# Two 64-row block sums of an fp32 decoder layer: one full fp32 product or two fp32r passes

## The chip, the cores and the metric

The kernel runs on one core of one Trainium2 chip. The metric is the device time of one execution in microseconds (us); lower is better.

## What is computed

One decoder layer for a sequence of 256 tokens with 2048 channels, all in float32: an input projection, sixteen RWKV-7 heads of width 64 beside eight differential attention heads, an output projection, a layer norm, an MLP of width 8192 with squared ReLU, and a second layer norm. Two lines of the RWKV part matter here, both of them sums over the 64 channels of a head:

```
kk    = heads(k * k_k)
kk    = kk / jnp.maximum(jnp.sqrt(jnp.sum(jnp.square(kk), -1, keepdims=True)), 1e-12)
bonus = (jnp.sum(r_h * k_h * r_k, -1, keepdims=True) * v_h).reshape(B, S, RWKV_WIDTH)
```

## The kernel before

Channels lie on the 128 partitions and tokens along the free axis. So one block of 128 channels holds two heads, and a sum over a head's channels is a TensorE product with a 128x128 matrix `BD` of ones in its two diagonal 64x64 blocks. `BD` is a part of the float32 constants `cst`.

The big products are done as fp32r products of parts. Each slab of weights (1 MB, 128x2048 float32) is loaded by SP's queue into one of four `stage` buffers. ScalarE copies it rounded to fp32r into `whi` (function `hi`), and VectorE writes the remainder `stage - whi` into `wlo` (function `lo`). TensorE then multiplies the activations' rounded part and remainder (`acts`) by `whi` in a product of 512 columns, and the rounded activations by `wlo` in one of 256 columns (function `both`). There are two `whi` and two `wlo` buffers, so `hi` of slab g waits until TensorE has used slab g-2 (`s_used`).

The change lies in the stage that projects k, r and v. It is a loop of NB // 2 = 4 turns `j`, each with three groups `c`: c = 0 projects 256 channels of k, c = 1 of r, c = 2 of v. A group is `pairs(...)`: two slabs of 16 pairs of products each, some 11.5 us of TensorE. Its sums go to two PSUM banks, and groups take turns between two sets of banks. After the pairs of c = 1 TensorE makes the block sum of the kk squares (`sqt`), and after the pairs of c = 2 that of the bonus terms (`rkt_`). Every engine works through its own list in program order:

- ScalarE, per group m: `hi(g + 2)`; for c = 1 the two squares into `sqt`; for c = 2 the square root of the kk sums into `inv`; then `low_copied(m)`, which waits for the end of the group's pairs and copies half of the sums into `hs`; `hi(g + 3)`; two scaled copies of `hs` into `krv`.
- VectorE, per group: for c = 0 (from j = 1) `bonus_and_kk(j - 1)`; for c = 1 the factors `ki` and `bt`; for c = 2 the products `rkt_`; then `lo(g + 2)`; for c = 2 the maximum with 1e-12 (L1619) and a reciprocal of half of `inv` (L1621); `halves_added(m)` (L1587), `lo(g + 3)` and the token shift into `krv` (L1628), which gives `s_free`.
- GpSimd, once per turn: four products (L2053 to L2057) as soon as kk is ready.

The order of these steps is written out by hand, with semaphores. TensorE's matmuls are nearly all recorded at L475, ScalarE's instructions at L1148, and `lo` at L1502, so rows are told apart by their tiles. A full float32 matmul appears as two records (x2).

Of the kernel before, what the change touches and what calls it, by code (L numbers as in the profile page):

```python
# [8 lines left out]
ALU = mybir.AluOpType  # L9
ACT = mybir.ActivationFunctionType  # L10
F32 = mybir.dt.float32
F32R = mybir.dt.float32r
# [4 lines left out]
P = 128  # L17
D = 2048
S = 256
# [86 lines left out]
def build(nc, t):  # L106

    ctx = ExitStack()
    with ctx:
# [3 lines left out]
        def at(name, slot, shape, dtype=F32, byte=0):  # L113
            return nc.alloc_sbuf_tensor_at(name, shape, dtype, offset=BASE + slot * SL_BYTES + byte)
# [4 lines left out]
        def sem(name):  # L119
            return ctx.enter_context(nc.semaphore(name))  # L120
# [26 lines left out]
        sqt = at("sqt", 13, [P, 2, S])  # L147
        inv = at("inv", 13, [P, 2, S], byte=2048)
        rkt_ = at("rkt_", 13, [P, 2, S], byte=4096)
        yt = at("yt", 13, [P, NB, S])  # L150
        oshi = [at("oshi0", 16, [P, NB, S], F32R), at("oshi1", 14, [P, NB, S], F32R)]
        oslo = [at("oslo0", 17, [P, NB, S], F32R), at("oslo1", 15, [P, NB, S], F32R)]
# [74 lines left out]
        ps = ctx.enter_context(nc.psum_tensor("ps", [P, 8, 512], F32))  # L227
# [18 lines left out]
        s_sq, s_ss, s_nrm = sem("kk_squares"), sem("kk_sums"), sem("kk_norms")  # L246
        s_ew = sem("elementwise_step")
        s_rk, s_bon, s_kk, s_pl = sem("bonus_terms"), sem("bonus_sums"), sem("kk_ready"), sem("pool_step")
        s_bonv = sem("bonus_ready")
        s_vdc = sem("v_copied")  # L250
        s_lamd = sem("lambda_step")
        s_lame = sem("lambda_exps")
# [40 lines left out]
        def col(v, n=0):  # L293
            return vec[:, v + n:v + n + 1]
# [9 lines left out]
        def f(ap):  # L304
            return ap.bitcast(F32)

        SU, IU, ID = cst[:, C_SU:C_SU + P], cst[:, C_IU:C_IU + P], cst[:, C_ID:C_ID + P]
        BD = cst[:, C_BD:C_BD + P]
# [6 lines left out]
        def banks(a, n=2, lo=0, hi=512):  # L315
            return ps[:, a:a + n, lo:hi]
# [156 lines left out]
        def _(pe):  # L473
            def mm(out, lhsT, rhs, start=True, stop=True):
                return pe.matmul(out, lhsT, rhs, start=start, stop=stop, skip_group_check=True)  # L475
# [11 lines left out]
            def pairs(b0, g, k0):  # L487
                for s in range(2):
                    halves_ready(g + s)
                    for j in range(8):  # L490
                        for fb in range(2):
                            last = both(b0 + fb, (k0 + s) % NHL, slice(256 * j + fb * P, 256 * j + fb * P + P), 8 * s + j)
                    last.then_inc(s_used, 1)
# [55 lines left out]
            for p in range(NB // 2):  # L549
# [4 lines left out]
                        last = mm(ps[:, 4 + p, o:o + P], sig[:, a, P * b:P * b + P], IU)  # L554
                last.then_inc(s_item, 1)

            for j in range(NB // 2):
                for c in range(3):
                    m = 3 * j + c
                    pe.wait_ge(s_free, m + 1)  # L560
                    pairs(2 * (m % 2), G_MIX + 2 * m, G_MIX + 2 * m)
                    if c == 1:
                        pe.wait_ge(s_sq, j + 1)
                        mm(ps[:, 4 + j % 2, :], BD, sqt[:, :, :]).then_inc(s_ss, 1)
                    if c == 2:
                        pe.wait_ge(s_rk, j + 1)
                        mm(ps[:, 6 + j % 2, :], BD, rkt_[:, :, :]).then_inc(s_bon, 1)

            def pairs_by_head(s, bk, left, right):

# [575 lines left out]
        def _(act):  # L1146
            def A(out, in_, func, **kw):
                return act.activation(out, in_, func, **kw)  # L1148
# [49 lines left out]
            for p in range(NB // 2):  # L1198
# [6 lines left out]
                  ACT.Exp, scale=-DECAY)  # L1205
                A(e2[:, two, :].rearrange("p b q -> p (b q)"), ps[:, 4 + p, :], ACT.Exp, scale=DECAY).then_inc(s_itemd, 1)

            def sines():
                act.wait_ge(s_ang, 9)
                A(sinb[:, :], angt[0][:, :], ACT.Sin).then_inc(s_sin, 1)  # L1210
                A(cosb[:, :], angt[2][:, :], ACT.Sin).then_inc(s_sin, 1)

            def low_copied(m):
                act.wait_ge(s_used, G_MIX + 2 * m + 2)
                act.wait_ge(s_free, m + 2)
                A(hs[:, :, :], banks(2 * (m % 2), 2, S, 2 * S), ACT.Copy).then_inc(s_plow, 1)

            for j in range(NB // 2):
                for c in range(3):
                    m = 3 * j + c  # L1220
                    g = G_MIX + 2 * m
                    if m == 0:
                        act.wait_ge(s_hi, g + 2)
                    hi(g + 2, g + 2)
                    if m == 0:
                        sines()
                    if c == 1:
                        act.wait_ge(s_free, m + 2)
                        for b in (2 * j, 2 * j + 1):
                            last = A(sqt[:, b % 2, :], krv[:, b, :], ACT.Square, scale=col(V_KK, b))  # L1230
                        last.then_inc(s_sq, 1)
                    if c == 2:
                        act.wait_ge(s_ss, j + 1)
                        A(inv[:, :, :].rearrange("p b q -> p (b q)"), ps[:, 4 + j % 2, :], ACT.Sqrt).then_inc(s_nrm, 1)
                    low_copied(m)
                    hi(g + 3, g + 3)
                    act.wait_ge(s_psum, m + 1)
                    for fb in range(2):
                        blk = NB * c + 2 * j + fb
                        last = A(krv[:, blk, :], hs[:, fb, :], ACT.Copy, scale=col(V_OMMU, blk))  # L1240
                    last.then_inc(s_mix, 1)
# [252 lines left out]
        def _(dve):  # L1494
            TTn, TS, STT = dve.tensor_tensor, dve.tensor_scalar, dve.scalar_tensor_tensor
# [45 lines left out]
            n = 0  # L1541
# [31 lines left out]
            def bonus_and_kk(j):  # L1573
# [3 lines left out]
                for b in (2 * j, 2 * j + 1):  # L1577
# [4 lines left out]
                TTn(krv[:, NB + 2 * j:NB + 2 * j + 2, :], krv[:, 2 * NB + 2 * j:2 * NB + 2 * j + 2, :],  # L1582
                    ps[:, 6 + j % 2, :].rearrange("p (b q) -> p b q", b=2), ALU.mult).then_inc(s_bonv, 1)

            def halves_added(m):
                dve.wait_ge(s_plow, m + 1)
                TTn(hs[:, :, :], banks(2 * (m % 2), 2, 0, S), hs[:, :, :], ALU.add).then_inc(s_psum, 1)  # L1587

            for j in range(NB // 2):
                two = slice(2 * j, 2 * j + 2)  # L1590
                K, R, E = krv[:, two, :], krv[:, NB + 2 * j:NB + 2 * j + 2, :], 5 * j
                for c in range(3):
                    m = 3 * j + c
                    g = G_MIX + 2 * m
                    if c == 0 and j:
                        bonus_and_kk(j - 1)
                    if c == 1:
                        for b in (2 * j, 2 * j + 1):
                            last = TS(ki[:, b, :], bt[:, b, :], col(V_KA, b), col(V_OMKA, b), ALU.mult, ALU.add)
                        last.then_inc(s_ew, 1)  # L1600
                        dve.wait_ge(s_ew, E + 1)
                        TS(bt[:, two, :], bt[:, two, :], -1.0, None, ALU.mult)
                        dve.wait_ge(s_free, m + 2)
                        TTn(ki[:, two, :], K, ki[:, two, :], ALU.mult).then_inc(s_ew, 1)
                    if c == 2:
                        dve.wait_ge(s_ew, E + 2)
                        dve.wait_ge(s_free, m + 2)
                        for b in (2 * j, 2 * j + 1):
                            last = STT(rkt_[:, b % 2, :], krv[:, NB + b, :], col(V_RK, b), ki[:, b, :], ALU.mult, ALU.mult)
                        last.then_inc(s_rk, 1)  # L1610
                        rt = kr[:, two, :, 1, :]
                        TTn(rt, rt, R.rearrange("p b (a q) -> p b a q", a=TT_), ALU.mult)
                    lo(g + 2, g + 2)
                    if m == 0:
                        dve.wait_ge(s_sin, 2)
                        TS(sinb[:, :], sinb[:, :], col(V_SIGN), None, ALU.mult).then_inc(s_tab, 1)
                    if c == 2:
                        dve.wait_ge(s_nrm, j + 1)
                        TS(inv[:, :, :], inv[:, :, :], 1e-12, None, ALU.max).then_inc(s_ew, 1)  # L1619
                        dve.wait_ge(s_ew, E + 3)  # L1620
                        dve.reciprocal(inv[:, 0, :], inv[:, 0, :]).then_inc(s_ew, 1)  # L1621
                    halves_added(m)
                    lo(g + 3, g + 3)
                    dve.wait_ge(s_mix, m + 3)
                    for fb in range(2):
                        blk = NB * c + 2 * j + fb
                        out = krv[:, blk, 1:S]
                        last = STT(out, hs[:, fb, 0:S - 1], col(V_MU, blk), out, ALU.mult, ALU.add)  # L1628
                    last.then_inc(s_free, 1)
# [43 lines left out]
            for q in range(1, 2 * N_QK):  # L1673
# [12 lines left out]
                if q % 2 == 0:  # L1686
                    rotary(q // 2 - 1)
            halves_added(N_MIX - 1)
            lo(G_VD + 1, G_VD + 1)
            rotary(N_QK - 1)  # L1690
# [466 lines left out]
```

## Time and profile before

| what | value |
|---|---|
| device time, median of 3 runs | 1275.46 us |
| lowest and highest run | 1270.92 and 1276.71 us |
| profiled execution, span from first to last instruction | 1273.7 us |
| profiled execution, device time beside its span | not listed apart from the three runs |
| share of the span busy: TensorE, VectorE, ScalarE, GpSimd | 98%, 59%, 45%, 6% |
| granted TensorE clock, mean | 0.997 |

The profiled execution's span lies 1.8 us below the median of the three runs and between the lowest and the highest, so a sum made against its rows can be carried to the median as it is. "PE" is TensorE's matmuls, "PEld" its weight loads, DVE is VectorE, ACT is ScalarE, POOL is GpSimd. A busy time of PE counts modelled ends of matmuls that overlap, so the time that a matmul takes from the array is read from start to start, not from its duration.

### The profile page before, as it was taken

How to read it: one execution, taken by the hardware profiler on the slowest of the kernel's cores; microseconds unless marked ns; L12 is line 12 of the kernel's file. 1: busy time of each engine (PE TensorE's matmuls, PEld its weight loads, DVE VectorE, ACT ScalarE, POOL GpSimd, SP SyncE). 2: the span in 40 equal slices, each digit the busy share in tenths (PEclk: the TensorE clock that was granted, in tenths of full speed). 3: DMA queues.
4: the chain of work that ended last, by engine and by line, in shares of the span. 5: the costliest groups of instructions: out<-in, count | busy, mean ns of one | idle time of the engine just before them, and what ended most of it. 6: DMA issues, size and time to landing. Idle time of an engine off the chain costs nothing.

```text
span 1273.7 us, 23270 instructions
## 1 busy us (share of the span) xinstructions
PE 1248.1 (98%) x9644; PEld 1043.1 (82%) x9644; DVE 755.2 (59%) x806; ACT 570.2 (45%) x605; POOL 74.6 (6%) x44
## 2 busy tenths in 40 slices
PE   6999999999999899999999999999999999999997
PEld 6888888888789778888888888888888888888885
DVE  4577878465766265765554545555555555655557
ACT  4754445555656134434334343343444444444442
POOL 0022112000000000056000000000000000000000
PEclk9999999999999999999999999999999999999999
DMA  8355565333421426635555555555575555555541
GB/s 334 129 190 181 176 227 201 106 134 101 166 100 39 152 93 222 262 100 193 174 193 186 179 196 179 183 196 173 191 264 188 181 191 198 198 190 182 190 163 66
DMA packets 33506, 221.88 MB, mean 174 GB/s; under 512 B 4621, under 2 KB 5005, under 8 KB 7582
## 3 DMA queue, kind: packets, MB, share of 16 engines
q1 hardware_dynamic: 33438, 220.88, 50.0%
q8 instruction: 54, 0.88, 0.3%
q14 instruction: 14, 0.11, 0.0%
HBM read 218.77 MB, written 2.10 MB: 173 GB/s over the span
## 4 chain that ended last, share of the span: by engine, by line
PE 55%; DVE 1%; ACT 0%; issue 0%; DVEq 0%
PE ps L475 55%; DVE stats L1894 0%; DVE xres L1893 0%; DVE xres L2015 0%; DVE xres L2013 0%; DVE xres L2003 0%; ACT xres L1148 0%; DVE xres L2007 0%; DVE moments L1897 0%; DVE moments L1904 0%; ACT moments L1148 0%; DVE shift_diag L2029 0%; DVE moments L1903 0%; DVEq L1887 0%
## 5 line engine op out<-in xcount | busy, mean ns | idle before, releaser
L1502 DVE TENSOR_TENSOR wlo<-stage,whi 128x2048 fp32r<-128x2048 f32 x186 | 435.4, 2341 | 397.4 <-ACT whi L1148 396.9
L475 PE MATMUL ps<-acts,whi 128*128 128x512 f32 (+1 forms) x1792 | 620.1, 395 | 13.7 <-DVE wlo L1502 11.4
L1148 ACT ACTIVATE whi<-stage 128x2048 fp32r<-128x2048 f32 x193 | 369.7, 1917 | 505.4 <-PE ps L475 502.4
L475 PE MATMUL ps<-acts,wlo 128*128 128x256 f32 (+1 forms) x1744 | 486.3, 279 | 0.0
L475 PEld LDWEIGHTS ps<-acts,whi 128*128 128x128 f32 x1792 | 335.2, 189 | 93.1 <-issue 17.9
L475 PEld LDWEIGHTS ps<-acts,wlo 128*128 128x128 f32 x1744 | 330.6, 190 | 1.9 <-issue 1.9
L475 PE MATMUL ps<-whi,shi 128*128 128x512 f32 x504 | 198.0, 393 | 0.0
L475 PE MATMUL ps<-wlo,shi 128*128 128x512 f32 x504 | 196.5, 390 | 0.0
L475 PE MATMUL ps<-whi,slo 128*128 128x512 f32 x504 | 196.3, 389 | 0.0
L475 PEld LDWEIGHTS ps<-whi,shi 128*128 128x128 f32 x504 | 94.6, 188 | 26.5 <-issue 5.9
L475 PEld LDWEIGHTS ps<-wlo,shi 128*128 128x128 f32 x504 | 94.6, 188 | 20.3
L475 PEld LDWEIGHTS ps<-whi,slo 128*128 128x128 f32 x504 | 94.7, 188 | 18.1
L475 PE MATMUL ps<-whi,oshi 128*128 128x512 f32 x128 | 51.8, 405 | 0.0
L475 PE MATMUL ps<-whi,oslo 128*128 128x512 f32 x128 | 50.4, 394 | 0.0
L475 PE MATMUL ps<-wlo,oshi 128*128 128x512 f32 x128 | 50.4, 393 | 0.0
L1859 DVE TENSOR_TENSOR slo<-hid,shi 128x512 fp32r<-128x512 f32 x64 | 43.9, 685 | 0.0
L475 PE MATMUL ps<-whi,acts 128*128 128x512 f32 x128 | 41.1, 402 | 0.0
L1148 ACT ACTIVATE shi<-hid 128x512 fp32r (+1 forms) x64 | 39.2, 613 | 1.1 <-PE ps L475 1.1
L1148 ACT ACTIVATE TM_TT<-ps 128x512 f32<-128x512 f32 x36 | 19.8, 596 | 41.7 <-PE ps L475 41.7
L1587 DVE TENSOR_TENSOR hs<-ps,hs 128x512 f32<-128x512 f32 x20 | 13.6, 679 | 37.5 <-ACT hs L1148 37.4
L1148 ACT ACTIVATE hs<-ps 128x512 f32<-128x512 f32 x20 | 12.0, 599 | 49.1 <-PE ps L475 49.1
L2082 POOL TENSOR_TENSOR xres<-xres,gain 128x512 f32<-128x512 f32 x2 | 2.5, 1288 | 517.0 <-DVE slo L1859 517.0
(227 smaller groups left out, 986.0 us busy)
## 6 DMA issues: line engine op xcount, KB each, us to landing
stage<-w_ff SPq DMA_DIRECT2D x128, 1024.0 KB, 4.9
stage<-w_in SPq DMA_DIRECT2D x51, 1024.0 KB, 5.0
stage<-w_out SPq DMA_DIRECT2D x16, 1024.0 KB, 5.0
xstage<-xT SPq DMA_DIRECT2D x4, 512.0 KB, 7.1
TM_TT<-eyes SPq DMA_DIRECT2D x4, 512.0 KB, 7.6
xres<-x SPq DMA_DIRECT2D x1, 2048.0 KB, 9.7
gain<-ln_gain SPq DMA_DIRECT2D x2, 1024.0 KB, 6.9
bias<-ln_bias SPq DMA_DIRECT2D x2, 1024.0 KB, 9.6
```

Of the source, the lines that this page charges most:

```text
L475: return pe.matmul(out, lhsT, rhs, start=start, stop=stop, skip_group_check=True)
L1148: return act.activation(out, in_, func, **kw)
L1502: TTn(wlo[k0 % NHL][:, :], stage[k0 % NST][:, :], f(whi[k0 % NHL][:, :]), ALU.subtract).then_inc(s_lo, 1)
L1587: TTn(hs[:, :, :], banks(2 * (m % 2), 2, 0, S), hs[:, :, :], ALU.add).then_inc(s_psum, 1)
L1859: TTn(slo[h][:, :, :], src, f(shi[h][:, :, :]), ALU.subtract).then_inc(s_alo, 1)
L2082: PT(x, x, gain2[:, quarter(q)], ALU.mult).then_inc(s_pg, 1)
```

## The change

Each of the eight block sums becomes two fp32r passes that add up in PSUM: `bdr` x rounded summands, then `bdr` x remainders. `bdr` is an fp32r copy of `BD`, made once by ScalarE before the loop. For each sum ScalarE makes the rounded summands `sumh` (128x512) and VectorE the remainders `suml` (128x512); both buffers are used by all eight sums in turn. TensorE waits for both parts ahead of each sum.

```diff
+        sumh = at("sumh", 12, [P, 2, S], F32R)
+        suml = at("suml", 12, [P, 2, S], F32R, byte=5120)
+        bdr = at("bdr", 12, [P, P], F32R, byte=7168)
@@ TensorE
+            def block_sums(bank, n):
+
+                pe.wait_ge(s_smh, n)
+                pe.wait_ge(s_sml, n)
+                mm(ps[:, bank, :], bdr[:, :], sumh[:, :, :], stop=False)
+                return mm(ps[:, bank, :], bdr[:, :], suml[:, :, :], start=False)
+
                     if c == 1:
-                        pe.wait_ge(s_sq, j + 1)
-                        mm(ps[:, 4 + j % 2, :], BD, sqt[:, :, :]).then_inc(s_ss, 1)
+                        pe.wait_ge(s_bdr, 1)
+                        block_sums(4 + j % 2, 2 * j + 1).then_inc(s_ss, 1)
                     if c == 2:
-                        pe.wait_ge(s_rk, j + 1)
-                        mm(ps[:, 6 + j % 2, :], BD, rkt_[:, :, :]).then_inc(s_bon, 1)
+                        block_sums(6 + j % 2, 2 * j + 2).then_inc(s_bon, 1)
@@ ScalarE
+            A(bdr[:, :], BD, ACT.Copy).then_inc(s_bdr, 1)
...
                         last.then_inc(s_sq, 1)
+                        act.wait_ge(s_sq, j + 1)
+                        if j:
+                            act.wait_ge(s_bon, j)
+                        A(sumh[:, :, :], sqt[:, :, :], ACT.Copy).then_inc(s_smh, 1)
                     if c == 2:
                         act.wait_ge(s_ss, j + 1)
                         A(inv[:, :, :].rearrange("p b q -> p (b q)"), ps[:, 4 + j % 2, :], ACT.Sqrt).then_inc(s_nrm, 1)
+                        act.wait_ge(s_rk, j + 1)
+                        A(sumh[:, :, :], rkt_[:, :, :], ACT.Copy).then_inc(s_smh, 1)
@@ VectorE
+            def summands_lo(src, n, spent):
+                dve.wait_ge(s_smh, n)
+                if spent is not None:
+                    dve.wait_ge(*spent)
+                TTn(suml[:, :, :], src[:, :, :], f(sumh[:, :, :]), ALU.subtract).then_inc(s_sml, 1)
+
                         dve.reciprocal(inv[:, 0, :], inv[:, 0, :]).then_inc(s_ew, 1)
+                        summands_lo(rkt_, 2 * j + 2, (s_ss, j + 1))
+                    if c == 1:
+                        summands_lo(sqt, 2 * j + 1, (s_bon, j) if j else None)
                     halves_added(m)
```

## Rows read from the trace of the kernel before

**Rows 1.** The page: busy time by engine, and the chain that ended last.

```profile
PE 1248.1 (98%) x9644; PEld 1043.1 (82%) x9644; DVE 755.2 (59%) x806; ACT 570.2 (45%) x605; POOL 74.6 (6%) x44
...
PE 55%; DVE 1%; ACT 0%; issue 0%; DVEq 0%
```

**Rows 2.** Busy time of each engine in the stage of the k, r and v projections.

```profile
core 0: us, PE busy (x) PEld busy (x) DVE busy (x) ACT busy (x) POOL busy (x), PEclk, DMA share, GB/s
45.00:195.00 150.00, 149.62 (x942) 126.55 (x941) 114.45 (x115) 72.73 (x79) 26.55 (x14) 1.00 0.54 183
```

**Rows 3.** Timeline of PE (start, length) around the first kk sum.

```profile
64.36 1.02 PE L475 MATMUL ps<-sqt,cst 128*128 128x512 f32 x2
64.82 0.79 PE L475 MATMUL ps<-acts,whi 128*128 128x512 f32 x1
65.45 0.28 PE L475 MATMUL ps<-acts,wlo 128*128 128x256 f32 x1
```

**Rows 4.** Timeline of PE in the MLP's second product: 15 matmuls of 512 columns.

```profile
1133.63 0.39 PE L475 MATMUL ps<-whi,slo 128*128 128x512 f32 x1
...
1136.80 0.39 PE L475 MATMUL ps<-whi,shi 128*128 128x512 f32 x1
```

**Rows 5.** Timeline of PE: the first and the last of the four bonus sums.

```profile
76.32 1.02 PE L475 MATMUL ps<-rkt__82,cst 128*128 128x512 f32 x2
...
183.43 1.02 PE L475 MATMUL ps<-rkt__82,cst 128*128 128x512 f32 x2
```

**Rows 6.** Timeline of DVE around the same two bonus sums; in brackets idle time before.

```profile
75.64 1.75 DVE L1621 RECIPROCAL inv<-inv 128x256 f32<-128x256 f32 x1
77.31 0.63 DVE L1587 TENSOR_TENSOR hs<-ps,hs 128x512 f32<-128x512 f32 x1
78.95 2.29 DVE L1502 TENSOR_TENSOR wlo<-stage,whi 128x2048 fp32r<-128x2048 f32 x1 [1.01 <-ACT whi L1148]
...
182.76 1.75 DVE L1621 RECIPROCAL inv<-inv 128x256 f32<-128x256 f32 x1
184.43 0.63 DVE L1587 TENSOR_TENSOR hs<-ps,hs 128x512 f32<-128x512 f32 x1
```

**Rows 7.** Timeline of ACT ahead of the first bonus sum's end.

```profile
74.26 0.60 ACT L1148 ACTIVATE inv<-ps 128x512 f32<-128x512 f32 x1
76.52 0.60 ACT L1148 ACTIVATE hs<-ps 128x512 f32<-128x512 f32 x1 [1.66 <-PE ps L475]
```

**Rows 8.** Line L1859: a remainder of 128x512, min/median/max in ns.

```profile
L1859 DVE TENSOR_TENSOR slo<-hid,shi x64: 683/685/687, 901.9 to 1249.8; 128x512 fp32r<-128x512 f32 x64
```

**Rows 9.** Timelines of ACT, DVE and PE around the second kk sum.

```profile
96.30 0.89 ACT L1148 ACTIVATE sqt<-krv,vec 128x256 f32<-128x256 f32 x2
...
96.66 2.28 DVE L1502 TENSOR_TENSOR wlo<-stage,whi 128x2048 fp32r<-128x2048 f32 x1
...
99.87 1.02 PE L475 MATMUL ps<-sqt,cst 128*128 128x512 f32 x2
```

**Rows 10.** Timelines of POOL, DVE and PE in the second turn's group c = 0.

```profile
84.91 1.30 POOL L2053 TENSOR_TENSOR bt<-bt,krv  x1 [84.46 <-DVE krv L1578]
86.16 3.34 POOL L2054 TENSOR_TENSOR kr<-kr,krv  x1
...
85.13 3.22 DVE L1502 TENSOR_TENSOR wlo<-stage,whi 128x2048 fp32r<-128x2048 f32 x1
...
88.16 0.28 PE L475 MATMUL ps<-acts,wlo 128*128 128x256 f32 x1
88.50 0.47 PE L475 MATMUL ps<-acts,whi 128*128 128x512 f32 x1
88.81 0.28 PE L475 MATMUL ps<-acts,wlo 128*128 128x256 f32 x1
```

**Rows 11.** A gap of PE in the recurrence, and the clock granted after it.

```profile
420.85 0.27 PE L475 MATMUL ps<-um,btm 64*64 64x64 f32 x2 [2.02 <-issue]
...
426.00:429.40 3.40, 3.40 (x22) 2.24 (x18) 1.29 (x2) 0.00 (x0) 0.00 (x0) 0.51 0.82 282
```

More of the change, by code:

```diff
@@ L249, in build @@
         s_bonv = sem("bonus_ready")
+        s_bdr, s_smh, s_sml = sem("block_sums_rounded"), sem("summands_rounded"), sem("summands_remainders")
         s_vdc = sem("v_copied")
```

## The prediction

> **What bounds the kernel.** I read the page first. TensorE is busy 98% of the span, no other engine above 59%, and the chain that ended last runs through PE for 55% of the span, with nothing else above 1% [rows 1]. What the change touches is a stage of 150 us; its busy times by window show PE at 149.62 us of 150.00 while DVE has 35 us free, ACT 77 us and POOL more, at a granted clock of 1.00, the 2.4 GHz level [rows 2]. So here a microsecond counts when it is TensorE's. Extra work on ACT or DVE costs nothing until TensorE has to wait for its result. Then I read the timelines around the sums, engine by engine: the question is not how busy DVE is on average but whether it has the remainders ready when TensorE comes to the sum.
>
> **What a full fp32 sum costs now.** The first kk sum starts at 64.36. The matmul of 512 columns behind it is followed by the one of 256 columns at 65.45 [rows 3]. A plain matmul of 512 columns takes (1136.80 - 1133.63) / 14 = 0.226 us from start to start [rows 4], so without the sum the 256-column matmul would have come at 64.59. The sum takes 65.45 - 64.59 = 0.86 us from the array: four times 0.215, nearly four plain passes, though the trace shows two records.
>
> **What two passes cost.** 2 x 0.226 = 0.45 us. I find no fp32r block sum in this trace, but the passes have the shape of [rows 4]. Saving: 0.86 - 0.45 = 0.41 us a sum, 8 x 0.41 = 3.3 us if nothing waits. Bounds: no saving (an fp32r pass here as long as half of the old product), or 0.43 (exactly half). I take 0.41, by the nearest row. The Trainium skill (FP8 and Floating Point Precision, TensorE Precision Notes) says that a true FP32 product takes four passes through the array. By that rule two passes save half of 0.86, 0.43 us a sum and 3.4 us in all; the trace agrees to 0.02 us. On passes alone the change is a gain of 0.26%; the rule tells nothing of the two waits.
>
> **The copy of BD.** One ACT copy of 128x128 ahead of the loop, in a stretch in which ACT waits for PE before its next `hi`. Bound above by the copy of 128x512, 0.60 us [rows 7]; on the path: nothing. Uncovered it would delay the first `hi` by that much, once.
>
> **The kk sums (c = 1).** ACT adds a copy of 128x512 behind the squares, DVE a subtraction behind `lo(g + 2)`. Queued behind DVE's new wait are `halves_added` and `lo(g + 3)`. The tightest of the four turns is the second: the squares end at 96.30 + 0.89 = 97.19, and the copy (0.60) at 97.8. DVE's `lo` ends at 96.66 + 2.28 = 98.94, and the subtraction takes 0.685 [rows 8], to 99.62. TensorE comes to the sum at 99.87 [rows 9]. It is ready 0.25 us early, so these four sums bring their saving: 4 x 0.41 = 1.6 us. DVE stood idle there anyway until ACT's copy of the low halves, so `halves_added` isn't later.
>
> **The bonus sums (c = 2).** Here the order matters. The remainders are written behind `lo(g + 2)`, the maximum and a reciprocal of 1.75 us. TensorE is done with the pairs and comes to the sum at 76.32, but the reciprocal runs from 75.64 to 77.39, and the next DVE instruction starts at 77.31 [rows 5, 6]. The last turn has the same distances: sum at 183.43, next DVE instruction at 184.43; all four turns show 1.0 us. So the subtraction starts 1.0 us after TensorE wants its result, and takes 0.685: it ends at T + 1.68, with T the old start of the sum. Before, `rkt_` had been ready since long ahead, and the reciprocal hid behind the next group. Now four times TensorE stands still.
>
> The rounded part is not what is late: ACT ends the square root at 74.86, and its copy would end by 75.5, ahead of the copy of the low halves at 76.52 [rows 7].
>
> From the subtraction to TensorE's restart I look at the one place in the stage where PE waits for DVE: `lo` ends at 85.13 + 3.22 = 88.35, the matmul starts at 88.50 and the next one 0.31 later, not 0.226 [rows 10]. That is 0.15 + 0.08 us for a restart. The bounds are nothing and 0.23; I take 0.2. New cost of a bonus sum from T: 1.68 + 0.2 + 0.45 = 2.33 us, in place of 0.86. Loss: 1.47 us each, 5.9 us for four.
>
> What is late next: `halves_added(m)` moves from 77.31 to 78.0 and ends at 78.6. `lo(g + 3)` behind it started at 78.95 after an idle 1.01 us in wait for ACT's `hi` [rows 6], so it starts as before, and with it the token shift and kk. Nothing else moves, and TensorE has `lo(g + 2)` of its next group since 75.2. Without that idle time the 0.69 us would go to the next `lo`, not yet to TensorE, which wants that slab half a group later.
>
> **The group after it (c = 0).** `lo(g + 2)` took 3.22 us here, not 2.29, beside two POOL products (POOL's second took 3.34 where the first took 1.30), and TensorE waited: the step from 88.16 to 88.50 is 0.34, against 0.11 for a matmul of half 0.226 [rows 10]. That is 0.23 us in each of three turns. With TensorE 1.47 us later while kk and POOL keep their time, `hi` is released 1.47 us later and ends at about 86.35 (84.9 + 1.47), after POOL's second product has begun at 86.16. If `lo` then lasts 3.2 to 3.4 again it ends at 89.55 to 89.75, and TensorE wants it at 88.27 + 1.47 = 89.74. So most of the old wait is given back: between 0 and 3 x 0.23 = 0.7 us, I take 0.5. The Trainium skill (SBUF — State Buffer, SBUF: two separate sides) has VectorE and GpSimd take turns at a shared pair of ports, each for a whole instruction. By it `lo` would wait for POOL's second product, 1.3 us from 86.16 if undisturbed, and end at 87.46 + 2.29 = 89.75: the same answer.
>
> **Sum.** -1.6 (kk sums) + 5.9 (bonus sums) - 0.5 (the old waits) = +3.8 us. The ends of the unknowns: -1.6 + 4 x 1.27 - 0.7 = +2.8 with no cost of restart, and -1.6 + 4 x 1.5 = +4.4. The other 1079 us are not touched: they follow TensorE. Against the profiled execution: 1273.7 + 3.8 = 1277.5. It lies 1.8 us below the median, so the forecast is 1275.46 + 3.8 = 1279.3 us, +0.3%. No change that a measurement of this kernel tells from none: the three runs lie 0.45% apart, and I take 0.5% (6.4 us) as the limit.
>
> **Rivals.**
>
> 1. The saving comes whole: all eight sums are ready in time. Then 8 x -0.41 = -3.3 us: 1272.2 us, the other side. The place is the bonus sum. What decides is the time from TensorE's arrival to the end of the subtraction; the change as a whole gains if the standstill is under about 0.4 + (1.6 + 0.5) / 4 = 0.9 us, and it comes to 1.9. For it speaks that ACT and DVE are idle half of the time. Against it, the reciprocal ends 1.07 us after T in both of the turns shown, before any subtraction.
>
> 2. The clock falls in the standstills. Behind a stretch of the recurrence with a gap of 2.02 us the trace shows 3.4 us at a granted clock of 0.51, the 1.2 GHz level [rows 11], which costs 1.7 us. Four times that: +6.8, in all +10.6, 1286.1 us. For it: the gap has nearly the length of the new ones. Against it: there TensorE had small 64x64 products and a second gap before the clock fell; here it runs dense up to the wait and after it.
>
> 3. The kk sums wait too, if the two new instructions or their semaphores take over 0.25 us more than the rows say. At 0.5 us each: 4 x 0.5 = +2, 1281.3 us. Only the second turn is that tight.
>
> 4. An fp32r pass of the block sum costs as much as half of the old product in the array's time (no saving). Then the eight savings are lost, 3.3 us: +7.1, 1282.6 us. Against it, [rows 4].
>
> **Chances.** The forecast 0.76, rival 1 0.06, rival 2 0.07, rival 3 0.07, rival 4 0.04. The range: the runs of before lie 4.5 us below and 1.3 above their median, so a median of three can be off by some 3; around 1279.3 with ends at +2.8 and +4.4 that gives 1274 to 1283. I take 1273.5 to 1284.5, which takes in rivals 3 and 4. Faster by over 0.5% needs rival 1 and a low run: 0.03. Slower by over 0.5% (above 1281.8) comes from rivals 2 and 4, half of rival 3, and a high draw of the forecast: 0.07 + 0.04 + 0.03 + 0.06 = 0.20. Within: 0.77.
>
> **What would show it.** In the trace after: eight pairs of 512-column matmuls on `bdr`, 0.45 us of array time each; PE idle before the four on bonus terms for 1.7 to 1.9 us, released by DVE `suml`; none before the four on squares; DVE's `halves_added` of c = 2 0.69 us later but `lo(g + 3)` still waiting for ACT; the step of 0.34 before c = 1's first pair nearer to 0.11; clock 1.00 throughout the stage; the stage 3.8 us longer and all behind it merely moved. I am wrong if the subtraction runs ahead of the reciprocal's end, if the clock row of the stage falls under 1.00, or if a wait appears behind the stage.

## The result, and the profile after

The changed kernel takes 1280.04 us (median of 13 runs, 1278.57 to 1281.8); the kernel before, timed beside it, 1275.14 us (13 runs, 1267.47 to 1276.94). The ratio is 1.0043, with a 95% interval of 1.0032 to 1.0055: slower by 0.4%, less than the 0.5% set as the limit. The forecast was 1279.3 us.

The page of the changed kernel, busy time by engine:

```profile
span 1277.9 us, 23305 instructions
PE 1245.5 (97%) x9644; PEld 1042.8 (82%) x9644; DVE 755.7 (59%) x814; ACT 575.0 (45%) x614; POOL 71.6 (6%) x44
```

TensorE is busy 2.6 us less than in [rows 1] and the span is 4.2 us longer: it had less to do and stood still for longer. The waits of PE name a line that isn't there before (waiter, what it waited for, us in total, times, longest):

```profile
PE ps L479 <- DVE suml L1607: 6.4, 4, 1.6
```

Four waits of 1.6 us on the remainders. The timeline of PE at the first bonus sum, against [rows 5]:

```profile
75.42 0.28 PE L479 MATMUL ps<-acts,wlo 128*128 128x256 f32 x1
77.32 0.47 PE L479 MATMUL ps<-sumh,bdr 128*128 128x512 f32 x1 [1.61 <-DVE suml L1607]
77.62 0.40 PE L479 MATMUL ps<-suml,bdr 128*128 128x512 f32 x1
77.86 0.40 PE L479 MATMUL ps<-acts,whi 128*128 128x512 f32 x1
```

The last pair's 256 columns go in at 75.42, so TensorE comes to the sum at 75.54, 0.12 later, and starts it at 77.32: 1.78 us lost, of which the view calls 1.61 idle because it counts the modelled end of the matmul before. Then two passes, and the next group at 77.86: 2.32 us from arrival, where the full product took 0.86. DVE in the same stretch, against [rows 6]:

```profile
74.88 1.75 DVE L1645 RECIPROCAL inv<-inv 128x256 f32<-128x256 f32 x1
76.54 0.63 DVE L1607 TENSOR_TENSOR suml<-rkt__82,sumh 128x512 fp32r<-128x512 f32 x1
77.09 0.68 DVE L1611 TENSOR_TENSOR hs<-ps,hs 128x512 f32<-128x512 f32 x1
78.17 2.29 DVE L1520 TENSOR_TENSOR wlo<-stage,whi 128x2048 fp32r<-128x2048 f32 x1 [0.41 <-ACT whi L1158]
```

TensorE's wait lies under the second half of the reciprocal and the subtraction. The last line is the one to check for a knock-on: `lo` waits for ACT as before, only 0.41 us in place of 1.01. The rounded part was long there (timeline of ACT):

```profile
73.98 0.62 ACT L1158 ACTIVATE sumh<-rkt__82 128x512 fp32r<-128x512 f32 x1
75.74 0.60 ACT L1158 ACTIVATE hs<-ps 128x512 f32<-128x512 f32 x1 [1.13 <-PE ps L479]
```

And the first kk sum, on PE's timeline against [rows 3], with no wait:

```profile
63.86 0.28 PE L479 MATMUL ps<-acts,wlo 128*128 128x256 f32 x1
63.98 0.40 PE L479 MATMUL ps<-sumh,bdr 128*128 128x512 f32 x1
64.21 0.40 PE L479 MATMUL ps<-suml,bdr 128*128 128x512 f32 x1
64.44 0.39 PE L479 MATMUL ps<-acts,whi 128*128 128x512 f32 x1
```

**A ruler for the stage.** Single executions of one and the same kernel lie up to 12 us apart here (below), so a profile's span says little about a gain of 2 us. The stretch that the change touches can be measured by itself: from the start of the first kk sum to the first `bt,kr` product behind the last bonus sum. Before it goes from 64.36 [rows 3] to 190.62, after from 63.98 to 193.40 (PE's timelines; first line before, second after):

```profile
190.62 0.69 PE L475 MATMUL ps<-bt,kr 64*64 64x64 f32 x32
```

```profile
193.40 0.69 PE L479 MATMUL ps<-bt,kr 64*64 64x64 f32 x32
```

That is 126.26 us before and 129.42 after: +3.16 us. Below, "the stage" is this stretch.

### The profile page after: what moved, and what is told of

It is laid out like the page before. It is cut to its first block, busy times and chain, and to the rows that moved or that the text cites. A ratio compares the mean times of both kernels' runs of the same rounds, so it can differ in the third digit from the quotient of the medians.

```text
span 1277.9 us, 23305 instructions
## 1 busy us (share of the span) xinstructions
PE 1245.5 (97%) x9644; PEld 1042.8 (82%) x9644; DVE 755.7 (59%) x814; ACT 575.0 (45%) x614; POOL 71.6 (6%) x44
## 4 chain that ended last, share of the span: by engine, by line
PE 55%; DVE 1%; ACT 0%; issue 0%; DVEq 0%
PE ps L479 55%; DVE stats L1921 0%; DVE xres L1920 0%; DVE xres L2042 0%; DVE xres L2040 0%; DVE xres L2030 0%; ACT xres L1158 0%; DVE xres L2034 0%; DVE moments L1924 0%; DVE moments L1931 0%; ACT moments L1158 0%; DVE shift_diag L2056 0%; DVE moments L1930 0%; DVEq L1914 0%
```

## The experiments

### Where the loss is: one kind of sum at a time

`kk_sums_only`: the bonus sums stay full products.

```diff
-                        block_sums(6 + j % 2, 2 * j + 2).then_inc(s_bon, 1)
+                        pe.wait_ge(s_rk, j + 1)
+                        mm(ps[:, 6 + j % 2, :], BD, rkt_[:, :, :]).then_inc(s_bon, 1)
```

(and neither copy nor remainders for them; the semaphore counts follow)

> Only the four kk sums are two passes; the bonus sums stay full fp32 products, with no copy and no remainders for them. Theory: no wait on suml, 4 x -0.41 = -1.6 us against before, about 1273.5, the short waits beside GpSimd unchanged. Rival (the two-pass form costs something of its own): no gain or a loss.

`bonus_sums_only`: the kk sums stay full products.

```diff
-                        pe.wait_ge(s_bdr, 1)
-                        block_sums(4 + j % 2, 2 * j + 1).then_inc(s_ss, 1)
+                        pe.wait_ge(s_sq, j + 1)
+                        mm(ps[:, 4 + j % 2, :], BD, sqt[:, :, :]).then_inc(s_ss, 1)
```

(and neither copy nor remainders for the kk sums; the semaphore counts follow)

> Only the four bonus sums are two passes, with the remainders behind the reciprocal as in the changed kernel; the kk sums stay full fp32 products. Theory: the four waits of 1.8 us with the cheaper passes, 4 x 1.46 = +5.8, less 1.4 us of old waits beside GpSimd that go: +4.4 us by the trace's sum against before, or 1.6 us more than the changed kernel. Rival (half of the loss comes from the kk sums): about half of the changed kernel's +4.9, +2.5 us.

Measured: with the kk sums alone the ratio to before is 0.9975 (0.9956 to 0.9994), and the stage takes 188.12 - 63.52 = 124.60 us, 1.66 less than before, as 4 x 0.41 says. With the bonus sums alone the ratio is 1.0042 (1.0020 to 1.0064) and the stage 195.66 - 64.47 = 131.19 us, 4.93 more; the loss by ratio is 5.4 us, against 4.4 expected. Of the 0.5 us between 4.4 and 4.93 the expectation knew nothing; the last section finds it in matmuls that ran at a slower pace. The two parts add up to +3.27, and both together gave +3.16. So the whole loss is in the bonus sums, and the kk sums are a gain. The tile view of `suml` in the second run has no kk sums, and the same wait:

```profile
L1606 DVE TENSOR_TENSOR suml<-rkt__82,sumh x4: 627/628/629, 77.4 to 187.9; 128x512 fp32r<-128x512 f32 x4
...
  PE ps L479: 6.4, 4
```

### Why: the remainders first, and half of the reciprocal first

`remainders_first` moves one call. VectorE's work is the same.

```diff
                     if c == 2:
+                        summands_lo(rkt_, 2 * j + 2, (s_ss, j + 1))
                         dve.wait_ge(s_nrm, j + 1)
                         TS(inv[:, :, :], inv[:, :, :], 1e-12, None, ALU.max).then_inc(s_ew, 1)
                         dve.wait_ge(s_ew, E + 3)
                         dve.reciprocal(inv[:, 0, :], inv[:, 0, :]).then_inc(s_ew, 1)
-                        summands_lo(rkt_, 2 * j + 2, (s_ss, j + 1))
```

> The changed kernel with one step moved: VectorE writes the remainders of the bonus terms before the maximum and the reciprocal, straight after the first lo of the group. Theory (the reciprocal of 1.75 us ahead of the remainders makes TensorE stand still): the four waits of 1.6 to 1.8 us on suml are gone, each sum costs 0.45 us in place of 0.86, and the old short waits beside GpSimd's products (1.6 us in all) come back. Against before: 8 x -0.41 = -3.3 us, about 1271.8, ratio 0.997. Rival (it is ScalarE's rounded copy, or the passes and semaphores as such, that cost the time): the wait stays and the time is that of the changed kernel, about 1280.

Ratio to before 0.9965 (0.9945 to 0.9985). The timelines of DVE and PE at the first bonus sum:

```profile
74.78 0.69 DVE L1607 TENSOR_TENSOR suml<-rkt__82,sumh 128x512 fp32r<-128x512 f32 x1
75.39 0.42 DVE L1644 TENSOR_SCALAR inv<-inv 128x512 f32<-128x512 f32 x1
75.84 1.75 DVE L1646 RECIPROCAL inv<-inv 128x256 f32<-128x256 f32 x1
```

```profile
75.57 0.28 PE L479 MATMUL ps<-acts,wlo 128*128 128x256 f32 x1
75.69 0.40 PE L479 MATMUL ps<-sumh,bdr 128*128 128x512 f32 x1
75.93 0.40 PE L479 MATMUL ps<-suml,bdr 128*128 128x512 f32 x1
76.16 0.39 PE L479 MATMUL ps<-acts,whi 128*128 128x512 f32 x1
```

The remainders end at 75.47, 0.22 us ahead of TensorE; the reciprocal runs on beside the next group, as it did before. The stage takes 187.62 - 64.12 = 123.50 us, 2.76 under before and 5.92 under the changed kernel, for one line moved. It falls 0.5 short of the 3.3 expected; 0.4 of that is the old waits beside GpSimd, which came back longer, 2.0 us in all in place of 1.6. The rival of a late ScalarE copy is out: ACT's list was not touched.

`remainders_first_again` is the same kernel in another batch of runs.

> The kernel with only the remainders moved ahead of the reciprocal, a second time, beside the run above. Theory: the stage again 123.5 us, the time 3 us under before, ratio 0.9975. Rival (the ratio of 0.9965 was the draw of the runs): a ratio at or above 1 with the same stage.

The stage takes 187.43 - 63.91 = 123.52 us, to 0.02 us the same; the ratio is 0.9979 (0.9960 to 0.9999).

`split_reciprocal` gives a half dose.

```diff
-                        dve.reciprocal(inv[:, 0, :], inv[:, 0, :]).then_inc(s_ew, 1)
+                        dve.reciprocal(inv[:, 0, 0:P], inv[:, 0, 0:P])
                         summands_lo(rkt_, 2 * j + 2, (s_ss, j + 1))
+                        dve.reciprocal(inv[:, 0, P:S], inv[:, 0, P:S]).then_inc(s_ew, 1)
```

> The changed kernel with the reciprocal of the bonus group cut in two halves of 128x128, the second half behind the remainders. Same work. Theory: about 0.85 us less stands ahead of the remainders, so each of the four waits falls from 1.8 us to about 0.95, and the old waits beside GpSimd stay gone: 4 x -0.85 = -3.4 us against the changed kernel, about +1.5 us against before. Rival (a fixed cost of the wait or of the passes): as the changed kernel, +4.9 us.

Its timeline of DVE, and that of PE at the sum:

```profile
74.91 0.95 DVE L1645 RECIPROCAL inv<-inv 128x128 f32<-128x128 f32 x1
75.78 0.63 DVE L1607 TENSOR_TENSOR suml<-rkt__82,sumh 128x512 fp32r<-128x512 f32 x1
76.32 0.94 DVE L1647 RECIPROCAL inv<-inv 128x128 f32<-128x128 f32 x1
```

```profile
75.46 0.28 PE L479 MATMUL ps<-acts,wlo 128*128 128x256 f32 x1
76.55 0.47 PE L479 MATMUL ps<-sumh,bdr 128*128 128x512 f32 x1 [0.81 <-DVE suml L1607]
```

0.80 us less ahead of the remainders (0.95 in place of 1.75), and the wait falls from 1.61 to 0.81 (0.69 in the second turn). The stage takes 189.96 - 64.01 = 125.95 us, 3.47 under the changed kernel (expected 3.4). The ratio to before is 1.0007 (0.9989 to 1.0025). The wait became shorter by as much as was taken away ahead of the remainders.

### The same cause from TensorE's side

`sum_half_a_group_later` leaves VectorE's order alone and moves the first three bonus sums on TensorE, between the two slabs of the next group.

```diff
-            def pairs(b0, g, k0):
+            def pairs(b0, g, k0, between=None):
                 for s in range(2):
+                    if s and between:
+                        between()
...
+                    late = (lambda: bonus_sum(j - 1)) if c == 0 and j else None
+                    pairs(2 * (m % 2), G_MIX + 2 * m, G_MIX + 2 * m, late)
...
-                    if c == 2:
+                    if c == 2 and j == NB // 2 - 1:
```

> The changed kernel with VectorE's order left alone, but TensorE makes the first three bonus sums between the two slabs of the next group, about 6 us later; the fourth stays where it was. Theory (TensorE comes to the sum 1.8 us before the remainders are written, nothing else): three of the four waits vanish, the fourth stays. From the first kk sum to the first level product the stage then takes 126.26 us (before) - 4 x 0.41 - 3 x 0.41 + 1.46 = 124.9 us, plus up to 0.5 if the waits beside GpSimd grow; total about 1274, ratio 0.999. Rival (the two passes with a switch of operands, or a late ScalarE copy, cost the time wherever the sum stands): the stage stays near 129.4 us.

One wait of 1.6 us on `suml` is left, the fourth, and the stage takes 190.21 - 64.65 = 125.56 us, 3.86 under the changed kernel and 0.16 over the upper end of what was expected. The ratio to before is 0.9991 (0.9967 to 1.0014). The passes cost nothing extra where the sum stands; what cost time was being asked for too early.

### The old waits beside GpSimd

In the runs without a standstill at the bonus sum and with GpSimd's start left alone, a short wait for `lo` stands ahead of group c = 1. In `remainders_first` it is 0.6 us in three turns (87.14 to 87.87 on PE's timeline, a step of 0.73 where 0.12 is due).

`gpsimd_one_step_later_on_before` changes the kernel before by one wait on GpSimd:

```diff
                 pool.wait_ge(s_kk, j + 1)
+                pool.wait_ge(s_bonv, j + 1)
```

> The kernel before, with one wait added on GpSimd: its products of a turn start once VectorE has also written the bonus values, so that VectorE's next lo starts ahead of them. The block sums are untouched. Theory (the 1.6 us of short waits in the stage come from lo standing behind GpSimd's products): lo of group c = 0 falls from 3.2 to 2.3 us and most of the 1.6 us goes: the stage from 126.3 to about 125.0 us. Rival (those waits have another cause, or GpSimd's products only collide with the next lo instead): the stage stays within 0.3 us of 126.3.

The timelines of DVE and POOL in the second turn's c = 0, against [rows 10]:

```profile
84.59 2.29 DVE L1502 TENSOR_TENSOR wlo<-stage,whi 128x2048 fp32r<-128x2048 f32 x1
```

```profile
85.03 3.01 POOL L2054 TENSOR_TENSOR bt<-bt,krv  x1 [84.57 <-DVE krv L1582]
```

Now `lo` starts first and takes its 2.29 us, and GpSimd's product takes 3.01 in place of 1.30. The stage takes 187.99 - 63.82 = 124.17 us, 2.09 under before, 0.5 more than the 1.6 of the waits (the last section says where that lies); ratio 0.9965 (0.9945 to 0.9985). The Trainium skill (SBUF — State Buffer, SBUF: two separate sides) has VectorE and GpSimd share a pair of ports, which whoever starts first has for a whole instruction. The traces agree: `lo` still had 1.85 us to run when GpSimd's product began, and 1.85 + 1.30 = 3.15 us, where the product took 3.01.

`remainders_first_gpsimd_later` puts this wait into `remainders_first`.

> The kernel with the remainders of the bonus terms ahead of the reciprocal, and GpSimd one step later as well. Theory: both gains add up: 123.5 us of stage less the 2.0 us of waits that stood beside GpSimd there, about 121.7 us; the total about 5 us under before, ratio 0.996. Rival (GpSimd's later products hit the second lo of the group): no better than the remainders first alone, 123.5 us.

No gain: 188.19 - 63.87 = 124.32 us, ratio 0.9986 (0.9965 to 1.0007). The waits of PE say why:

```profile
PE ps L479 <- DVE suml L1607: 1.4, 3, 0.6
```

It is the kk sums' remainders now that are late, in three turns. TensorE comes to the sum earlier than it did, and VectorE's list up to the remainders of c = 1 is as long as before.

`three_steps_together` then moves VectorE's factors `ki` and `bt` (1.16 us) from c = 1 to c = 0, where DVE had idle time.

> Remainders of the bonus terms first, GpSimd one step later, and VectorE's factors ki and bt (1.16 us) moved from group c = 1 to the idle time of c = 0 ahead of the copy of the low halves. Theory (with the first two alone the remainders of the kk squares came up to 0.6 us late in three turns, since GpSimd's product stretches the token shift of c = 0 to 1.9 us): the moved 1.16 us makes them early again, and the stage falls from 124.3 us to 126.26 - 8 x 0.41 - 2.1 = 120.9 us. Rival (the wait moves on to the next lo or to GpSimd's products): 122 us or more.

A miss: 191.04 - 64.46 = 126.58 us, ratio 1.0037 (1.0016 to 1.0058). The timelines of DVE and PE in the second turn:

```profile
84.84 2.29 DVE L1520 TENSOR_TENSOR wlo<-stage,whi 128x2048 fp32r<-128x2048 f32 x1
87.05 2.69 DVE L1636 TENSOR_SCALAR ki<-bt,vec 128x256 f32<-128x256 f32 x2
89.77 1.56 DVE L1639 TENSOR_SCALAR bt<-bt 128x512 f32<-128x512 f32 x1
91.25 0.68 DVE L1611 TENSOR_TENSOR hs<-ps,hs 128x512 f32<-128x512 f32 x1
```

```profile
94.78 0.47 PE L479 MATMUL ps<-acts,whi 128*128 128x512 f32 x1 [1.17 <-DVE wlo L1520]
```

The two factors take 2.69 us there, not 0.73, and `bt` 1.56, not 0.43, since GpSimd's four products run in just that idle time. The sum of the low halves and the next `lo` come late, and TensorE waits for `lo`, by 1.3 to 1.6 us in three turns. The idle time was idle only in the view of one engine.

`factors_a_turn_ahead` writes the factors of turn j + 1 in c = 1 of turn j, behind the kk remainders, where GpSimd is done.

```diff
+                        if ahead:
+                            factors(j + 1, E + 3)
```

> Remainders of the bonus terms first, GpSimd one step later, and VectorE's factors ki and bt of turn j + 1 written in group c = 1 of turn j, behind the remainders of the kk squares, where GpSimd has long been done. Theory (in the run with the first two steps the kk remainders came late by 0.5 to 0.7 us in three turns; with the factors in c = 0 they collided with GpSimd): nothing but short waits is left, the stage takes about 122 us, 4 us under before, ratio 0.997. Rival (1.16 us more in c = 1 makes the copy of the low halves and the next lo late): 124 us or more.

The stage takes 186.20 - 63.90 = 122.30 us, 3.96 under before, and no wait of PE for `suml` or of more than 0.15 us for `lo` is left. The median is 1268.41 us against 1273.26 for before in the same batch, ratio 0.9977 (0.9955 to 0.9999). Against before that is a gain, though its interval ends just under 1; against the changed kernel the stage is 7.1 us shorter. By ratio it can't be told from `remainders_first`; by the stage it is 1.2 us shorter.

### The changed kernel again

> The changed kernel as it is, beside the run above on one chip. Theory: the stage from the first kk sum to the first level product again takes 129.4 us, 3.2 us more than before, and the time is 3 to 5 us over before. Rival (the 4.9 us between the medians hold a cost outside the stage that the trace's 3.2 us don't show): the stage the same and the rest of the span again over 1 us longer than before at the same pace of the MLP.

The stage takes 193.56 - 64.12 = 129.44 us, again 3.2 over before; the ratio is 1.0037 (1.0014 to 1.0061). What lies behind the stage, to the end of the span, is 1269.7 - 193.56 = 1076.1 us. At the same pace of the MLP (below) it is 1074.9 to 1078.7 us in the six other kernels, all of which have the same instructions there. So the rest of the span is not longer in this execution of the changed kernel. The two clusters of times (last section) can also be compared each with its own: the median of the lower cluster is 1272.2 us against 1269.3 for before, that of the upper one 1279.3 against 1276.1, so +2.9 and +3.2 us. The rival falls.

## Why the prediction was right, and where a term was mis-sized

- **Passes.** Forecast 0.45 us for two, 0.86 for the full product. Measured 64.44 - 63.98 = 0.46, and `kk_sums_only` shows the saving by itself: 1.66 us for four.
- **The kk sums in time.** Right: no wait in the changed kernel, in any of four turns. All four had 0.5 us to spare, more than the 0.25 forecast for the tightest: in the second turn the remainders ended at 99.11 + 0.68 = 99.79 and the sum started at 100.34.
- **The bonus sums late.** Right in cause and size: 2.32 us from arrival to the next group, forecast 2.33. The restart, forecast 0.2, was 0.15 (77.17 to 77.32) and 0.07. The order on VectorE as the cause is shown three ways: order, dose, and the sum moved on TensorE.
- **What is late next.** Right: `lo(g + 3)` still waits for ACT.
- **The old waits given back: the term that was mis-sized.** The prediction counted three, 0.7 us at most, and took 0.5. The steps of PE's timeline before show five: beside those of c = 0 (0.23, 0.20 and 0.20) two in the middle of c = 1, and behind each the 0.08 us of a restart, 1.6 us in all. One of the two in c = 1, in the kernel before:

```profile
129.59 0.28 PE L475 MATMUL ps<-acts,wlo 128*128 128x256 f32 x1
129.99 0.47 PE L475 MATMUL ps<-acts,whi 128*128 128x512 f32 x1
```

  a step of 0.40 where 0.12 is due. After the change two traces of them are left, 0.2 us at most together. So 1.4 us came back, not 0.5, and the sum is -1.6 + 5.9 - 1.4 = +2.9 in place of +3.8; the trace shows +3.16. The rest of 0.3 us stands in one stretch, from the second bonus sum to the third kk sum, where TensorE worked without a wait but at a slower pace (last section). The prediction had no term for that.
- **The total.** The medians differ by 4.9 us, 1.7 more than the stage. In the profiled pair the span grew by 4.2: 3.16 in the stage, -0.38 ahead of it, 1.42 behind it. Of that, 1.1 lies in the last products (timelines of PE, first before, second after):

```profile
1265.86 4.39 PE L475 MATMUL ps<-gain,shift_diag 128*128 128x512 f32 x6 [4.17 <-DVE shift_diag L2029]
```

```profile
1269.04 5.49 PE L479 MATMUL ps<-gain,shift_diag 128*128 128x512 f32 x6 [4.15 <-DVE shift_diag L2056]
```

  In both kernels they follow a standstill of over 4 us and ran partly at a granted clock of 0.50, the 1.2 GHz level (windows around them, after):

```profile
1269.00:1272.00 3.00, 2.96 (x4) 1.40 (x5) 2.96 (x5) 0.00 (x0) 0.00 (x0) 0.50 0.05 18
1272.00:1275.00 3.00, 2.53 (x3) 0.43 (x2) 1.48 (x3) 0.00 (x0) 0.00 (x0) 0.55 0.83 311
```

  But the 1.1 us doesn't belong to the change: the same products took 4.33 us in the second execution of the changed kernel, and 4.30 to 5.49 over all kernels. The stretch behind the stage takes 1081.3 to 1084.7 us over the six profiled executions of the slower pace (before 1083.1, after 1084.5), so 1.4 us is inside its scatter. In the batch of `changed_kernel_again` the clusters differ by 2.9 and 3.2 us, no more than the stage. The 1.7 us that the medians of the first batch show beyond the stage I therefore put down to the draw of the runs; what made them is not shown. So it is partly luck that 1280.04 lies so near the forecast of 1279.3: the stage came out 0.6 us under its term, and the 1.7 us beyond it, which nothing forecast, made up for that.
- **Rivals.** The clock did not fall in the standstills. The window of the stage after, against [rows 2]:

```profile
45.00:195.00 150.00, 143.55 (x868) 124.02 (x867) 113.67 (x123) 77.17 (x88) 22.50 (x14) 1.00 0.52 183
```

  PE's busy time is 6.1 us less with the four gaps in it, the granted clock is 1.00. Rivals 1, 3 and 4 did not happen.

## What to carry to other kernels

Work moved to an engine with idle time is free only if its result stands in that engine's list ahead of the moment at which the bound engine asks for it: look at the timeline of that moment, not at the busy share. A cheaper form of an operation that needs one more operand can cost more than it saves through that operand's place in the order, and one moved line can turn the loss into the gain. Before moving work into an idle gap, look at what else runs in that gap and slows that engine down (GpSimd beside VectorE here), and after each gain look which operand has become the late one.

## What the runs showed that was not expected

**Two paces of the same matmuls.** Executions of all these kernels fall in two clusters some 6 us apart, the kernel before included (from 1266.6 to 1278.2 us over all its runs). In the profiles nearly all of the difference sits in the first product of the MLP, which no edit touches: from the first transpose of the first norm's output to the first matmul of the second product it takes 372.7 to 373.1 us in six of them and 366.6 to 366.7 us in the other seven. The same 340 us of that product hold more instructions in the quick pace (windows, before and `kk_sums_only`; PE busy and count first):

```profile
560.00:900.00 340.00, 340.00 (x1926) 294.57 (x1925) 181.46 (x121) 130.09 (x91) 31.44 (x16) 1.00 0.54 185
```

```profile
560.00:900.00 340.00, 340.00 (x1961) 297.11 (x1960) 185.42 (x124) 131.92 (x92) 31.41 (x16) 1.00 0.54 188
```

1961 against 1926 matmuls at the same granted clock of 1.00, with no wait in either: every pair of matmuls takes 1.8% less. It is why changes of 2 to 4 us are told here by the stage in the trace and not by the medians alone.

The slower pace occurs in the stage as well, in stretches. Here are the first matmul behind the second bonus sum and the third kk sum after the change, and the second bonus sum and the third kk sum of `gpsimd_one_step_later_on_before`:

```profile
114.23 0.39 PE L479 MATMUL ps<-acts,whi 128*128 128x512 f32 x1
136.83 0.40 PE L479 MATMUL ps<-sumh,bdr 128*128 128x512 f32 x1
```

```profile
110.78 1.02 PE L475 MATMUL ps<-rkt__82,cst 128*128 128x512 f32 x2
133.83 1.02 PE L475 MATMUL ps<-sqt,cst 128*128 128x512 f32 x2
```

Between them lie 64 pairs with no wait in either: 22.60 us after, and 23.05 less the 0.86 of the full sum = 22.19 us, so 0.353 and 0.347 us a pair, the same two paces. What the pairs of the stage took beyond 0.347 us each, waits left out, adds up to 0.5 us before, 0.9 after (1.0 in its second execution), 1.1 in `bonus_sums_only` and nothing in `gpsimd_one_step_later_on_before`. That is the rest that the sums above left over: 0.3 to 0.4 us in the changed kernel, 0.5 in `bonus_sums_only`, and 0.5 gained with GpSimd's later start. In the kernel before, every slow stretch inside the stage begins right behind the restart from a short wait (88.50, 123.98, 159.73 and 165.75 on PE's timeline) and ends at the next sum or wait; behind the fifth restart, 129.99, TensorE ran at the quick pace. What chooses the pace was not tried. The stage agrees to 0.02 us in two pairs of executions, but because of these stretches it says little about a difference of under half a microsecond between two kernels.

**The price of a restart.** After a wait the first matmul of 512 columns takes 0.30 to 0.31 us to the next one in place of 0.23 (77.32 to 77.62 above), whatever was waited for.
